# The first adaLN quarter in two eighths of 256 columns, and other work moved around them at the head of a one-core layer

## The reference, cut to what matters

```
cond = silu(c)                                  # 1 x 2048
mod  = cond @ w_ada + b_ada                     # w_ada: 2048 x 18432, nine rows of 2048
u = rmsnorm(h, norm1_g) * (1 + sc1) + sh1       # 256 x 2048
a, b = split(u @ ffn1_w_in)                     # 2048 x 11264
h = h + 0.5 * gt1 * ((silu(a) * b) @ ffn1_w_out)
```

## Time and profile before

| | |
|---|---|
| median of 3 runs | 2096.5 us (2096.43 to 2097.93) |
| the profiled execution's own time | 2095.69 us |
| its span | 2093.9 us |
| PE busy | 2063.7 us, 99% |
| DVE busy | 1622.7 us, 77% |
| ACT busy | 1051.2 us, 50% |
| PE clock over the span | 0.997 of 2.4 GHz |

### The profile page before, as it was taken

One profiled execution on the slowest core, in us unless ns is written; L12 is line 12 of the kernel. 1 busy time (PEld: TensorE's weight loads), 2 busy tenths in 40 slices (PEclk: granted clock), 3 DMA queues, 4 the chain that ended last, 5 costly groups with the idle time before them and its releaser, 6 DMA issues.

```text
span 2093.9 us, 24080 instructions
## 1 busy us (share of the span) xinstructions
PE 2063.7 (99%) x9369; PEld 1706.9 (82%) x9369; DVE 1622.7 (77%) x2000; ACT 1051.2 (50%) x1390; POOL 4.5 (0%) x22
## 2 busy tenths in 40 slices
PE   7999999999999999999999999999999999999998
PEld 6788888888888878888888888888888888888887
DVE  6987997988789888787777799778875566755666
ACT  4577434565346555446444675554443444434444
POOL 0000000000000000000000000000000000000000
PEclk9999999999999999999999999999999999999999
DMA  9998998998899878975555689667665555555554
GB/s 348 387 385 302 330 335 310 339 339 291 297 336 331 294 247 295 321 278 163 166 169 168 215 289 345 216 225 288 230 206 196 197 187 199 190 193 200 186 177 161
DMA packets 249601, 540.79 MB, mean 258 GB/s; under 512 B 11920, under 2 KB 14352, under 8 KB 248720
## 3 DMA queue, kind: packets, MB, share of 16 engines
q1 hardware_dynamic: 249104, 539.12, 72.6%
q10 hardware_dynamic: 384, 0.13, 0.0%
HBM read 537.10 MB, written 2.11 MB: 258 GB/s over the span
## 4 chain that ended last, share of the span: by engine, by line
PE 91%; DVE 4%; DMA 1%; ACT 1%; issue 1%; SPq 1%; ACTq 0%; DVEq 0%
PE pa L695 15%; PE pb L695 15%; PE pa L698 15%; PE pa L697 15%; PE pb L698 15%; PE pb L697 15%; DVE lo L1635 1%; DMA raw<-in_ffn_w_in_dram 1%; ACT hi L1156 1%; DVE ada_acc L1655 1%; DMA ada_s<-in_w_ada_dram 1%; DVE proj L2224 0%; SPq L485 0%; DVE ada_acc L1733 0%; SPq L516 0%
## 5 line engine op out<-in xcount | busy, mean ns | idle before, releaser
L1156 ACT CAST hi<-raw 128x1024 fp32r<-128x1024 f32 (+1 forms) x732 | 750.6, 1031 | 906.4 <-PE pb L698 431.3
L1635 DVE TENSOR_TENSOR lo<-raw,hi 128x1024 fp32r<-128x1024 f32 (+1 forms) x732 | 867.3, 1197 | 405.6 <-ACT hi L1156 403.8
L695 PE MATMUL pa<-hi,act_hi 128*128 128x512 f32 x1024 | 404.4, 395 | 7.6 <-DVE act_lo L1702 4.4
L695 PE MATMUL pb<-hi,act_hi 128*128 128x512 f32 x1024 | 401.8, 392 | 0.0
L698 PE MATMUL pa<-hi,act_lo 128*128 128x512 f32 x1024 | 399.5, 390 | 0.0
L697 PE MATMUL pa<-lo,act_hi 128*128 128x512 f32 x1024 | 399.3, 390 | 0.0
L698 PE MATMUL pb<-hi,act_lo 128*128 128x512 f32 x1024 | 398.7, 389 | 0.0
L697 PE MATMUL pb<-lo,act_hi 128*128 128x512 f32 x1024 | 398.5, 389 | 0.0
L1733 DVE SCALAR_TENSOR_TENSOR ada_acc<-ada_w,cond,ada_acc 128x1024 f32<-128x1024 f32 (+1 forms) x240 | 275.1, 1146 | 6.5 <-DVE ada_acc L1733 0.5
L695 PEld LDWEIGHTS pa<-hi,act_hi 128*128 128x128 f32 x1024 | 192.8, 188 | 51.4 <-DVE act_lo L1702 5.4
L698 PEld LDWEIGHTS pa<-hi,act_lo 128*128 128x128 f32 x1024 | 192.7, 188 | 40.5
(11 more groups left out here) (335 smaller groups left out, 1548.3 us busy)
## 6 DMA issues: line engine op xcount, KB each, us to landing
raw<-in_ffn_w_in_dram SPq DMA_DIRECT2D x176, 1024.0 KB, 4.9
ada_w<-in_w_ada_dram SPq DMA_DIRECT2D x224, 512.0 KB, 6.0
raw<-in_ffn_w_out_dram SPq DMA_DIRECT2D x64, 1024.0 KB, 5.1
raw<-in_w_in_dram SPq DMA_DIRECT2D x64, 1024.0 KB, 5.1
ada_s<-in_w_ada_dram SPq DMA_DIRECT2D x64, 512.0 KB, 10.9
raw<-in_ffn_w_out_dram SPq DMA_DIRECT2D x32, 768.0 KB, 4.3
raw<-in_w_out_dram SPq DMA_DIRECT2D x16, 1024.0 KB, 5.7
raw<-in_w_att_up_dram SPq DMA_DIRECT2D x8, 1024.0 KB, 5.1
```

The lines of the kernel that those rows point to most:

```text
L695: pe.matmul(ps, a_hi[:, k0 + kk, tok], w_hi, start=start and kk == 0, stop=False, skip_group_check=on)
L1156: act.copy(hi_of(ph, i, j, half)[:, 0:n, 0:w], raw[:, j % RING, 2 * half:2 * half + n, 0:w])\
L1635: dve.tensor_tensor(lo[:, j % RING, s, 0:w], raw[:, j % RING, s, 0:w], hi_of(ph, i, j, half)[:, 0:n, 0:w].bitcast(F32), ALU.subtract)\
```

## The change

- **Quarter 0 comes as two stages, eighths of 256 shift and 256 scale columns**, each over all 16 depth tiles, in 8 transfers of 512 KB (`load_start_half`), whose rows are 1 KB long instead of 2 KB. Stage 0 (k-tiles 0 and 1) has tiles 2, 3, 12, 13 on PE; stage 1 (k-tiles 2 and 3) has 6, 7, 14, 15. Both stages use the same room; SP's loads of stage 1 wait until stage 0's tiles there are used.
- **Order of the units.** Position 0's first half, position 1's first half (the other bank), then their second halves (`first_unit`), then as before. Chunks 0 and 1 are loaded in halves.
- **PE.** Norm groups 0 to 4, tiles 12 and 13, the flush of stage 0 (4 transposes), groups 5 to 7, units 0 and 1, then stage 1's four tiles and flush, then unit 2. The flush of quarter 1 comes behind unit 15.
- **DVE.** It squares half of x itself. All of stage 1's tiles stand behind `lo` of unit 1, before `lo` of unit 2. Quarter 1's tiles are behind units 4, 6, 7, 9, 11, 13 and (four) 15.
- **ACT.** c is loaded first, transposed and given to silu alone; the square-root table is loaded early; the three last copies to `n_t` stand between the first roundings; the small rows (L535 to L539) are issued from ACT's queue behind units 24 to 27.
- **x** is loaded in four column blocks.

```diff
-    ON_PE = ((2, 3, 9, 12), (), (), ())
+    ON_PE = ((2, 3, 12, 13), (6, 7, 14, 15), (), (), ())
+    def first_unit(s):
+        return (s % 2, s // 2) if s < 4 else (s // 2, s % 2)
...
+            def load_start_half(e, a):
+                c4, m = a // 2, a % 2
+                if e == 1:
+                    by_dve, by_pe = s_used(0, 4 * (c4 + 1))
+                    sp.wait_ge(s_dve, by_dve)
+                    sp.wait_ge(s_pe, by_pe)
+                sp.dma_start(ada_s[:, c4, m, :].rearrange("p (k n) -> p k n", k=4),
+                             wada_rows[:, 4 * c4:4 * c4 + 4, (SH1, SC1)[m], e * (NC // 2):(e + 1) * (NC // 2)])\
+                    .then_inc(ada_s_in[a], 16)
...
-            sp.dma_start(h[:, :, :], x_tok).then_inc(x_in, 16)
-            for k in range(8):
-                load_start(k)
+            for b in range(4):
+                sp.dma_start(h[:, :, b * NC:(b + 1) * NC], x_tok[:, :, b * NC:(b + 1) * NC]).then_inc(x_in[b], 16)
+            for a in range(8):
+                load_start_half(0, a)
...
+            for pos in range(2):
+                load_half(pos, 0, raw_in[pos])
+            for a in range(8):
+                load_start_half(1, a)
+            for pos in range(2):
+                load_half(pos, 1, second_in[pos])
+            load_first(2)
+            load_start(8)
+            load_first(3)
+            load_start(9)
+            load_start(10)
+            load_first(4)
+            for m in range(3):
                 load_start(11 + m)
-                load_first(4 + m)
+                load_first(5 + m)
+            load_start(14)
+            for m in range(16):
+                load_start(15 + m)
+                load_first(8 + m)
...
-                start_open()
-                start_tile(2, False)
-                start_tile(3, False)
-                for g in range(KD // 2):
+                start_open(0)
+                start_tile(0, 2, False)
+                start_tile(0, 3, False)
+                for g in range(5):
                     norm_group(g)
-                    if g == 3:
-                        start_tile(9, False)
-                start_tile(12, True)
-                start_flush(0)
-                for pos in range(32):
+                start_tile(0, 12, False)
+                start_tile(0, 13, True)
+                start_flush_half(0)
+                for g in range(5, KD // 2):
+                    norm_group(g)
+                for s in range(64):
+                    pos, half = first_unit(s)
...
+                    if s == 2:
+                        start_open(1)
+                        for kt in ON_PE[1]:
+                            start_tile(1, kt, kt == ON_PE[1][-1])
+                        start_flush_half(1)
...
+                    if s == 15:
+                        start_flush(1)
...
                 start_tiles(0, range(2, KD))
-                start_bias()
+                start_bias(0)
                 start_mod(0, 0)
                 start_affine()
                 lo_unit(0)
                 start_lo(0)
+                lo_unit(1)
+                start_tiles(1, range(KD))
+                start_bias(1)
                 start_mod(0, 1)
-                lo_unit(1)
+                lo_unit(2)
                 start_lo(1)
-                lo_unit(2)
                 lo_unit(3)
```

More of the change, by code:

```diff
@@ L172, in first_chunk, with s_used @@
         return q, r // 2, (r // 2 if q % 2 == 0 else 3 - r // 2), r % 2
-    def s_used(q, n):
-        on_dve = sum(kt not in ON_PE[x // KD] for x in range(KD * q + n) for kt in (x % KD,))
-        return on_dve, KD * q + n - on_dve
+    def first_unit(s):
+        return (s % 2, s // 2) if s < 4 else (s // 2, s % 2)
+    def s_used(stage, n):
+        on_dve = sum(kt not in ON_PE[x // KD] for x in range(KD * stage + n) for kt in (x % KD,))
+        return on_dve, KD * stage + n - on_dve
     PIECES = [(g, (0,)) for g in range(4)] + [(g, (1,)) for g in range(4)] + [(g, (0, 1)) for g in range(4, 8)]
@@ L294, in build @@
         rows_in = sem("rows_in")
-        x_in = sem("x_in")
+        x_in = [sem(f"x_in{b}") for b in range(4)]
+        c_in = sem("c_in")
+        c_tr = sem("c_tr")
+        second_in = [sem(f"second_in{j}") for j in range(2)]
         fin_in = sem("fin_in")
@@ L446, in hi_of @@
                 return hi_a[:, :, :] if k == 3 else hi_b[:, k, :, :]
+            if ph is plan["ffn1_in0"] and j < 2:
+                return hi[:, 2 * half + j, :, :]
             return hi[:, (2 * j + half) % 4, :, :]
@@ L926, in first_body @@
                         transposes(idx - 1)
[L927 to L933, removed]
+                    if 0 < q < 3 and (idx, ab, half) == (3, 1, 0):
+                        start_flush(q + 1)
+                    if idx == 0 and ab == 0:
+                        pe.wait_ge(xt_lo, 2 * q + half + 1)
+                    unit(ph, 0, pos, half, 4 * q + 2 * half, 2, act_hi, act_lo, bank,
+                         q == 0 and half == 0, half == 1, on=True, order=s)
+                    if s == 15:
+                        start_flush(1)
             def ffn(f):
@@ L1143, in link, with split @@
                 act.wait_ge(act_step, steps[0])
-            def split(ph, i, j, half, n, w=NC):
-                u = 2 * (ph.c0 + ph.per * i + j) + half
+            def split(ph, i, j, half, n, w=NC, order=None):
+                u = 2 * (ph.c0 + ph.per * i + j) + half if order is None else order
+                if order is not None and order in (2, 3):
+                    act.wait_ge(second_in[j], 16)
                 if half == 0:
@@ L1313, in first_body, with x_copy @@
             def first_body(ph):
-                for g in range(KD // 2):
+                def x_copy(g):
                     act.wait_ge(xt_mm, g + 1)
@@ L1318, in first_body @@
                         .then_inc(n_t_ok, 1)
+                for g in range(5):
+                    x_copy(g)
                 def affine(g):
-                    act.wait_ge(n_t_ok, KD // 2)
+                    act.wait_ge(n_t_ok, g + 1)
                     act.wait_ge(gain_ok, g + 1)
@@ L2173, in _ @@
                 dve.memset(inv_f[:, i:i + 1], float(np.float32(ROPE_THETA ** (-i * 2.0 / ROT))))
+            for b in (0, 1):
+                dve.wait_ge(x_in[b], 16)
+                for tt in range(TT):
+                    cols = h[:, tt, b * NC:(b + 1) * NC]
+                    ins = dve.scalar_tensor_tensor(out=part[:, b, 0, tt, :], in0=cols, scalar=1.0, in1=cols,
+                                                   op0=ALU.mult, op1=ALU.mult, accum_out=ss4[:, tt, b:b + 1])
+            link(ins)
+            dve.wait_ge(cond_ok, 1)
+            start_tiles(0, range(0, 2))
             dve.wait_ge(par_tr, 1)
```

181 lines of the change are left out of this document (105 added, 76 removed).

## The result

The changed kernel is slower: 2103.99 us against 2096.47, a ratio of 1.0036 (95% interval 1.0026 to 1.0047). On another chip, where it served as a control, it was 1.0032 (1.0021 to 1.0044). I had forecast 2098.5, with a range up to 2103.0.

What follows compares the result with a forecast made beforehand. PE's back-to-back work from position 8 on bounds the kernel, so its start decides: 89.5 instead of 87.49. Profiled 2095.69 + 2.0 = 2097.7, with the runs' median 0.8 above: 2098.5 us; 8-in-10 range 2094.0 to 2103.0.

Steps and rivals of the forecast that it cites:

- main line: Prologue to position 8: unit 0 8.5 us earlier, stage 1 loses it, position 8 2.0 us later; 2098.5 us, chance 0.42.
- rival (a): Wait after quarter 1's flush, before position 8: clock falls there too, a further 2.0 us, 2100.5; chance 0.24.
- Statistics and first groups: Before unit 0: `dg` at 16.3 instead of 18.27, five norm groups in 7.1 us, ending at 23.4.
- Stage 1's tiles: DVE between units 1 and 2: 12 half-width tiles at 0.81 each, 9.4 us, until 40.2; unit 2 at 45.1.
- The clock at unit 2: Unit 2 starts at half clock after the longer idle stretch: 2.0 us lost, bounds 0 and 3.4.
- The flush behind unit 15: Quarter 1's flush with no unit behind it: 4.3 us to position 8, of which 3.2 idle.
- The one row that I held against the rule: Against a clock fall before position 8: the earlier 82 to 88 stretch, idle parts 0.94 and 1.2, kept 1.00.
- Rival (b): First five groups and tiles 12 and 13 stay at half clock: unit 2 slips 3.2, 2101.7 us; chance 0.12.
- Rival (c): Stage 1 does not hold PE, units run through, DMA bounds: position 8 at 83.8, 3.7 earlier, 2092.8 us; chance 0.11.
- The price that the sum had for the transfers: Stage 1's pieces: 512 KB with 1 KB rows in 1.49 us at 351 GB/s, last piece at 35.9.
- 0.10 for a time below 2092.3: Whole kernel: chance 0.10 of being faster by over 0.2%, only if stage 1 does not hold PE, with something more.
- the small rows fall where they cost nothing: Small row transfers, 2.7 us, move to around position 12, where chunks lie about 8 us ahead: nothing, bounded by 2.7.

Runs made afterwards that it cites:

- e13: Changed kernel with DVE's two copies of the small parameters in front of its first two tiles instead of behind them; 2101.18 us, 1.0024.
- e5: Changed kernel with most shift and scale columns of stage 1's tiles 1 to 15 left out, output not the layer's; 2098.55 us, 1.0016.
- e3: Changed kernel with 8 extra dense matmuls, result not read, on PE behind stage 1's flush, before unit 2; 2100.63 us, 1.0024.
- e1: Changed kernel with the flush of quarter 1 before unit 15 instead of behind it; 2100.15 us, 1.0023.
- e4: Changed kernel with the four small row transfers issued by SP again, behind chunk 4's load, instead of by ACT; 2102.41 us, 1.0033.
- e2: Changed kernel with 14 extra dense matmuls, result not read, on PE behind the flush of quarter 1; 2102.76 us, 1.0033.
- e6: Changed kernel with quarter 1's flush before unit 15 and 8 unread filling matmuls before unit 2; 2098.05 us, 1.0010.
- e7: Kernel before with 8 extra unread matmuls of 128 columns on PE behind quarter 0's flush, before unit 0; 2095.98 us, 0.9999.
- e10: Kernel before with only the four small row transfers moved, on SP, behind the last tile of quarter 3; 2094.94 us, 0.9994.
- e8: Kernel before with 8 unread matmuls before unit 0 and the small row transfers moved behind quarter 3's last tile; 2094.42 us, 0.9992.
- e9: Kernel before with every edit of the change but the split into stages and what hangs on it; 2096.15 us, 1.0001.
- e11: Kernel before with every edit but the split, plus 8 unread filling matmuls before unit 0; 2095.44 us, 0.9997.

## Why the prediction was wrong

It forecast a position 8 at 89.5, 2.0 us late; it came at 92.95, 5.5 late, and the clock fell once more behind it. The mechanism of its main line was right: unit 0 gained much (8.5 said, 6.7 seen), stage 1 on DVE took all of it, unit 2 at half clock, an uncovered flush, no wait for a chunk. Its premise held too, that the start of position 8 decides: from the second chunk of quarter 1 to the end the seventeen traces took 2000.5 to 2002.3 us. What failed were sizes, one wait and the weight of rival (a). From 89.5 to 92.95:

- **Statistics and first groups, 1.8 us.** The step had PE's own two tiles done before `dg`, at 16.3. Their start was not looked at: PE waits for both parameter copies before anything of ffn1, and the change puts these copies behind DVE's first two tiles, which wait for the first pieces. PE began its tiles at 15.47 and the groups at 18.88, 2.6 behind the 16.3 said. About 0.8 of that is `dg`, ready only at 17.1 because the first pieces landed at 13.2 and not at 12.3. By luck the groups took 6.46 and not 7.1, which hid 0.6. The wait for the copies is one that the change adds, and I named nothing behind it; e13 took it away: the groups began 2.2 earlier, at 16.64, and unit 0 came 1.6 earlier, at 29.96 against the predicted 29.7. It is the step of the prediction that was wrong, not only mis-sized.
- **Stage 1's tiles, 0.8 us.** 12 tiles took 10.2, not 9.4: consecutive half-width operations start 0.88 us apart, where I had added to the 0.75 of the earlier trace rows the gap of 0.06 between full-width ones. The price of halving is therefore 2 x 0.88 against 1.34. e5 confirmed that this arithmetic, and not the pieces, held unit 2: 3.7 earlier without it.
- **The clock at unit 2, 0.65 us.** 5.3 us of dense work at half clock instead of 4: 2.65 lost for 2.0. e3 removed it. The step laid the fall to the longer idle stretch; in the trace the clock was down at 39.5, before PE idled.
- **The flush behind unit 15** took 4.40, for 4.3: right. e1 removed the wait.
- The rest of the 3.45, 0.2, is in smaller steps.

Then **rival (a)**, to which I gave 0.24, happened: 3.36 us idle after 1.03 of transposes, and position 8 at 0.50 for 3.4 us, 1.7 lost (2.0 said). By the rule of the Trainium skill ("TensorE: Matmul & The Clock Gate", "Why this matters for your kernels": leave no long idle gap between bursts) this case was the likelier, and the traces agree at this place: the clock was low behind all six waits of 3.35 to 3.43 before position 8 (the changed kernel twice, e3, e4, e5, e13) and behind none of the ten that were 0.60 to 0.90; filling the long one kept it (e2), as did shortening it (e1). The 3.46 of the earlier trace rows is weaker support: the clock was down 0.6 us after that gap opened, behind a tile of one-column matmuls and the transposes. The one row that I held against the rule had idle parts of at most 1.2 us, which is no counterexample to a gap three times as long. Of the 1.7 us lost at position 8, 1.4 remain net, because the chunk takes 5.79 and not 5.44 where the clock holds (before, e1, e6). 3.45 + 1.4 is 4.9; with the predicted 2.0 that is 6.9 of the span's 7.6. The other 0.7 lies in small steps behind it, 0.3 of it in the wait for `act_lo` near 787 (2.29 for 1.99).

Rival (b), half clock through the first groups, did not occur: the groups took 6.46, less than the 7.1 I had. (That part of them runs at half clock is read from their pace, 6.13 against 3.86 for the same 32 matmuls in the earlier trace rows; the windows give the granted clock as 1.00 there.) Rival (c) did not occur. The price that the sum had for the transfers held: 1 KB rows moved at 350 GB/s (the first window of the changed kernel below, in stage 1's pieces; the second takes in some 2 KB rows at its end), against 389 for 2 KB rows, so the line rate from 512 bytes on that the Trainium skill, "DMA: Bandwidth & Descriptors", "Specifications", gives was not reached. The last piece was waited for until 38.0 (e5, and e13, where PE waits for it), not 35.9 as said, and nothing depended on it in the changed kernel. One chance did not follow from the sums: 0.10 for a time below 2092.3 is nearly all of (c), whose own figure was 2092.8.

```profile
25.00:36.00 11.00, 9.70 (x68) 8.72 (x66) 8.53 (x16) 4.76 (x8) 0.00 (x0) 1.00 1.10 350
28.50:37.50 9.00, 7.70 (x45) 6.53 (x43) 8.15 (x14) 3.11 (x5) 0.00 (x0) 1.00 1.09 356
```

The sentence that the small rows fall where they cost nothing held (e4). What I did not say is the other half, which e7 and e10 show: before, those rows sat in the one stream that bounded position 8. So the start of unit 0 was never worth its microseconds alone: without moving them, even 2 us of clock regained at unit 0 came out as 0.5 at position 8.

## What to carry to other kernels

Splitting a first stage to start earlier pays only until the second half is due: add up the second half's own chain (its tiles on the busiest engine, then flush, sums, gains, activations) from the end of the first, and compare with where that unit stood before. Here 16.3 us passed between unit 0 and unit 2 for 5.6 us of work. A reordered prologue can make an engine wait for something small that used to be ready early; list for each engine its first waits and who now stands in front of them. And when a change opens an idle gap of the size seen here (3.4 us) between dense matmuls, or a stretch of one-column matmuls and transposes of some microseconds, charge the work behind it with the low clock; the cheapest cures are to leave one unit of work behind the flush, or to fill the gap. Last, a transfer taken out of one place of a busy stream can be paid for at another, as in e10: look for the first chunk behind its new place.

## What the runs showed of the hardware that was not expected

Matmuls whose result nobody reads raise the clock as well as useful ones: 8 of them moved the return to 2.4 GHz from 5.3 us behind unit 2's start to just before it (e3).

The clock can go down under a busy PE. In ten of the eleven traces with the split it did so between 38.3 and 41.8, after the two units of dense work and during the one-column matmuls (in the eleventh, e5, which has few of them, at 40.4, 0.5 us behind the transposes); in the changed kernel PE's rows show no pause from the units to 42.2.

The clock can also fall at an idle time that leaves it alone in another execution. In the next feed-forward stage PE idles 2.0 us for `act_lo`; the traces of the kernel before (1.99 idle) and of the changed kernel (2.29) keep 1.00 there, while that of e13 (an edit 700 us earlier) shows, in PE's timeline and in two windows, 3 us at 0.50 behind the same idle time:

```profile
785.73 0.76 PE L730 MATMUL pa<-hi,act_hi 128*128 128x512 f32 x1 [2.01 <-DVE act_lo L1880]
```

```profile
780.00:785.00 5.00, 3.72 (x18) 2.95 (x16) 4.68 (x12) 3.88 (x9) 0.00 (x0) 1.00 0.47 141
786.00:789.00 3.00, 3.00 (x8) 2.33 (x8) 3.00 (x10) 2.15 (x7) 0.00 (x0) 0.50 0.88 323
```

It is there in the traces of e1, e2, e8, e9, e11 and e13, 6 of 17. Half of its 3.4 us, 1.7, is lost in the stretch itself; from the second chunk of quarter 1 to the end these six traces are 1.1 us longer in the mean than the ten others (2002.1 against 2001.0, e10 left out for its late rows). Differences of 1 to 2 us between versions of this kernel can come from this alone; that the edits caused it is not shown.
